# Delta-rule pairs: the sums of squared outputs of two heads as two products with 64 columns of ones, on the two halves of one bank

## The chip, the cores and the metric

The kernel runs on one core of one Trainium2 chip. The metric is the device time of one execution in microseconds (us). PE is TensorE (PEld its weight loads), DVE is VectorE, ACT is ScalarE, POOL is GpSimd, SP is SyncE. Everything is float32 in and out; most weight products are done as three products of rounded high parts and remainders.

## The reference, cut to what matters

The whole program is a transformer block with a state-space mixer, then two blocks with other mixers. The change is in one place of the second part, the gated delta rule (`gdn_mixer`): 8 heads of 128 channels, 512 tokens. After the recurrence each head's output is normalised over its 128 channels, multiplied with a gate, and projected:

```python
def rms_norm_2(x, g):
    xf = x.astype(jnp.float32)
    y = xf * lax.rsqrt(jnp.mean(xf * xf, axis=-1, keepdims=True) + EPS_2)
    return (y * g.astype(jnp.float32)).astype(x.dtype)
...
    o = gated_delta_rule(q, k, v, g, beta).astype(hn.dtype)
    o = rms_norm_2(o, norm_g) * jax.nn.silu(gate)
    return o.reshape(b_, s_, GDN_WIDTH) @ w_out
```

The sum over 128 channels of the squared outputs of a head, its logarithm, and exp(-0.5 log), which is the reciprocal root, are what the change touches.

## The kernel before, in words

Activations stand transposed: 128 channels on the partitions, 512 tokens along the free axis, so one head's output is one 128x512 tile and a sum over channels is a product with a 128x128 matrix of ones, which leaves the sum on all 128 partitions. PSUM `ps` has 8 banks of 128x512 float32. Each engine has its own written instruction list; the engines meet only by semaphores, and each list runs in the order in which it is written.

The delta rule (`pe_mixer2`, `act_mixer2`, `dve_mixer2`, `pool_mixer2`) works on pairs of heads, p = 0 to 3; x = 2p + j is the head. A pair goes through six levels n = 0 to 5 of a triangular inverse, then through four chunks of the recurrence. At each level PE makes the U product (L1514), ACT copies it to `em` (L1732), PE makes the D product (L1549), which has `em` as its weights, and DVE subtracts (L1968) and transposes (L1971). Between these PE does pieces of weight work from a stream (`spare`; L1364 to L1366 for gates, L1375 to L1377 for output parts).

The outputs of pair p end in the banks MOVED = (3, 0). ACT copies each to `v2` (L1778) and squares it into `o_sq[j]` (L1779). The rest belongs to the next pair's levels:

- n = 0: PE multiplies each `o_sq[j]` with 128 columns of ones into bank MOVED[j] (L1520); ACT takes the logarithm back into `o_sq[j]` (L1704, `out_log_sum`), and then casts a weight unit (`act_round`, L413).
- n = 1: PE's transposes of v go into the same banks and wait for the logarithms.
- n = 2: ACT takes the exponential (L1708, `out_rstd`), then scales `kb` (L1719). At n = 3 it copies `em` again.
- n = 3 and 4: DVE uses `o_sq[j]` (L1939, then L1942, `out_gated`).

For the last pair there is no next one, and the same steps stand in a tail: PE L1609, between output products (L1396 to L1398, `pe_out_unit`); ACT a cast L413, L1704, L1708, another cast L413, then `mid2_hi` (L1712); DVE L1939 and L1942 for both heads, then `mid2_lo` (L1947). PE's third output unit of the tail waits for that `mid2_lo`. Whenever ACT has cast a weight unit, POOL computes its remainder (L2639).

`Chain.link(ins)` makes an instruction count on a semaphore of its engine and lets the engine wait for it. The same kernel already has sums with 64 columns of ones for the norms of q and k: `square_sum`, L1446, with ACT's logarithm L1651 and exponentials L1656.

Of the kernel before, what the change touches and what calls it, by code (L numbers as in the profile page):

```python
# [21 lines left out]
ALU, ACT, AX = mybir.AluOpType, mybir.ActivationFunctionType, mybir.AxisListType  # L22

P = 128
# [11 lines left out]
EPS_1, EPS_2 = 1e-5, 1e-6  # L36
# [158 lines left out]
def build(nc, units, x_t, p_t, vectors, constants, rel_table, out_t):  # L195
# [10 lines left out]
    with ExitStack() as ctx:  # L206
# [1197 lines left out]
        def pe_mixer2(pe, w):  # L1404
# [33 lines left out]
            def square_sum(m):  # L1438
# [7 lines left out]
                    last = nc.tensor.matmul(ps[64 * half:64 * half + 64, SUM_BANK[m // 2 % 4], :], ones[:, 0:64], n_sq[:, m % 4 + half, :], start=True, stop=True)  # L1446
                last.then_inc(s_nsum, 2)

            for u in range(N_QKV):
                slot = (n0 + u) % W_SLOTS  # L1450
                pe.wait_ge(s_wlo, n0 + u + 1)
                pe.wait_ge(s_free, b0 + u + 1)
                for k in range(DK):
                    if u == 0:
                        pe.wait_ge(s_xlo, w.tiles - DK + k + 1)
                    hi, lo = w_hi[:, slot, k * P:(k + 1) * P], w_lo[:, slot, k * P:(k + 1) * P]
                    out = ps[:, u % 4, :]
                    nc.tensor.matmul(out, hi, x_hi[:, k, :], start=(k == 0), stop=False)  # L1458
                    nc.tensor.matmul(out, hi, x_lo[:, k, :], start=False, stop=False)  # L1459
                    last = nc.tensor.matmul(out, lo, x_hi[:, k, :], start=False, stop=(k == DK - 1))  # L1460
                last.then_inc(s_used, 1)
                if u == 0:
                    pe_norm_sum(pe, w, 4)
                    pe.wait_ge(s_sum2, 8)
                    nc.tensor.matmul(ps[:, 5, :], ones, sum2[:, :], start=True, stop=True).then_inc(s_msum2, 1)
                    w.norms += 1
                if 5 <= u < 20 and u % 2:
                    if u == 5:
                        pe.wait_ge(s_rstd, w.norms)
                    square_sum(u - 5)  # L1470
                if u == 6:
                    pe.wait_ge(s_ga2, 2)
                    for m in range(NB):
                        last = nc.tensor.transpose(ps[:, 7, m * 64:m * 64 + 40], g_row[:, m * P:(m + 1) * P], ident[0:40, 0:40])
                    last.then_inc(s_gcolp, 1)
                if u == 20:
                    for j in range(2):
                        decay_broadcast(0, j)
                if u == 21:
                    pe.wait_ge(s_nrs, 4)  # L1480
                    nc.tensor.matmul(ps[:, 6, 0:32], ident[:, P - 1:P].to_broadcast([P, P]), cols2[:, :, 0:8], start=True, stop=True).then_inc(s_gtot, 1)
                if u == 22:
                    for j in range(2):
                        beta_broadcast(0, j)
                if u == 23:
                    for j in range(2):
                        products_of_k(0, j)
# [5 lines left out]
            for p in range(4):  # L1493
# [7 lines left out]
                for n in range(6):  # L1501
                    b = 2 << n
                    if n == 5:
                        for j in range(2):
                            pe.wait_ge(s_gd, level(p, 4, j))
                            for c in range(NB):
                                last = nc.tensor.transpose(ps[:, LEVEL[j], c * P:(c + 1) * P], gw["tt"][j][:, c, :], ident)
                            last.then_inc(s_gtp, 1)
                    for j in range(2):
                        pe.wait_ge(s_gao, level(p, n, j))  # L1510
                        pe.wait_ge(s_gtm, level(p, n, j))
                        for c in range(NB):
                            for side in range(2):
                                last = nc.tensor.matmul(level_out(j, 0, b, c, side), gw["ao"][j][:, c, 64 * side:64 * side + 64],  # L1514
                                                        halves(gw["tm"][j][:, c, :], b, 0), start=True, stop=True)
                        last.then_inc(s_gup, 1)
                    if n == 0 and p:
                        for j in range(2):
                            pe.wait_ge(s_osq, 2 * p - 1 + j)
                            nc.tensor.matmul(ps[:, MOVED[j], :], ones, o_sq[j][:, :], start=True, stop=True).then_inc(s_osum, 1)  # L1520
                        spare(stream, "b")
                    for j in range(2):
                        x = 2 * p + j
                        if n == (1 if p else 2):
                            if p:
                                pe.wait_ge(s_oln, x - 1)
                            else:
                                pe.wait_ge(s_free, b0 + 29)
                            for c in range(NB):
                                cols = slice(c * P, (c + 1) * P)  # L1530
                                last = nc.tensor.transpose(ps[:, MOVED[j], cols], v2[:, x, cols], ident)
                            last.then_inc(s_gvt, 1)
                        if n == (2 if p else 3):
                            pe.wait_ge(s_gvb, x + 1)
                            for c in range(NB):
                                cols = slice(c * P, (c + 1) * P)
                                last = nc.tensor.transpose(ps[:, MOVED[j], cols], qk2[:, 8 + x, cols], ident)
                            last.then_inc(s_gkt, 1)
                        if p < 3:
                            if n == 3:  # L1540
                                decay_broadcast(p + 1, j)
                    if n == 1:
                        spare(stream, "U1")
                    for j in range(2):
                        pe.wait_ge(s_gz, level(p, n, j))
                        pe.wait_ge(s_gu, level(p, n, j))
                        for c in range(NB):
                            for side in range(2):
                                last = nc.tensor.matmul(level_out(j, 1, b, c, side), gw["em"][j][:, c, 64 * side:64 * side + 64],  # L1549
                                                        halves(gw["tt"][j][:, c, :], b, 1), start=True, stop=True)  # L1550
                        last.then_inc(s_gdp, 1)
                    spare(stream, f"D{n}")
# [51 lines left out]
            w.square_layer(2)  # L1604
            w.square_layer(2)
            pe_out_unit(pe, n_t, TAIL2[0], (0,), False, mids)
            for j in range(2):
                pe.wait_ge(s_osq, 7 + j)
                nc.tensor.matmul(ps[:, MOVED[j], :], ones, o_sq[j][:, :], start=True, stop=True).then_inc(s_osum, 1)  # L1609
            pe_out_unit(pe, n_t, TAIL2[0], (1, 2, 3), False, mids)  # L1610
            for d in range(2):
                pe.wait_ge(s_fill[d], TASKS_BEFORE[4] // 2)
# [5 lines left out]
        def act_mixer2(act, w, gain):  # L1618
# [80 lines left out]
            def round_at(n):  # L1699
                act_round(act, 0, first + n + AHEAD)  # L1700

            def out_log_sum(p, j):
                act.wait_ge(s_osum, 2 * p + j + 1)
                nc.scalar.activation(o_sq[j][:, :], ps[:, MOVED[j], :], ACT.Ln, bias=EPS_2, scale=1.0 / P).then_inc(s_oln, 1)  # L1704

            def out_rstd(p, j):
                act.wait_ge(s_oln, 2 * p + j + 1)
                nc.scalar.activation(o_sq[j][:, :], o_sq[j][:, :], ACT.Exp, scale=-0.5).then_inc(s_ors, 1)  # L1708

            def out_hi(p, j):  # L1710
                act.wait_ge(s_on, 2 * p + j + 1)
# [11 lines left out]
            for p in range(4):  # L1723
                for n in range(6):
# [7 lines left out]
                        nc.scalar.activation(halves(wide(gw["em"][j]), b, 0), level_out(j, 0, b), ACT.Copy).then_inc(s_gu, 1)  # L1732
                    for j in range(2):
                        x = 2 * p + j
                        if n == 0 and p:
                            out_log_sum(p - 1, j)
                        if n == (1 if p else 2):
                            if x == 0:
                                act.wait_ge(s_convact, 36)
                            act.wait_ge(s_gvt, x + 1)  # L1740
                            for c in range(NB):
                                last = nc.scalar.activation(gw["vb"][j][:, c, :], ps[:, MOVED[j], c * P:(c + 1) * P], ACT.Copy, scale=cols2[:, c, 32 + x:33 + x])
                            last.then_inc(s_gvb, 1)
# [3 lines left out]
                        conv_silu(23)  # L1747
                    if n == 2:
                        if p:
                            for j in range(2):  # L1750
                                out_rstd(p - 1, j)
                            k_scaled(p, 0, "kb", g_exp)
                    if n == 3:
                        if not p:
# [26 lines left out]
            n_t = w.unit  # L1781
            layers = [w.square_layer(2), w.square_layer(2)]
            act_round(act, 0, n_t + AHEAD)
            for j in range(2):
                out_log_sum(3, j)
            for j in range(2):
                out_rstd(3, j)
            act_round(act, 0, n_t + 1 + AHEAD)
            for j in range(2):
                out_hi(3, j)  # L1790
# [1017 lines left out]
```

## Time and profile before

| | |
|---|---|
| time, median of 3 runs | 2560.58 us (2556.51 to 2561.22) |
| the profiled execution's own time | 2560.09 us |
| its span, first to last instruction | 2558.3 us |
| granted TensorE clock, mean | 0.996 |
| PE busy | 2510.6 us, 98% of the span |
| DVE, ACT, POOL busy | 1084.4, 1096.8, 1053.2 us (42%, 43%, 41%) |
| the delta-rule pairs and their tail | about 1225 to 1465 us in the span |

PE is busy nearly always; the other engines are busy less than half the time. Where PE waits, the time is lost; where another engine waits, usually not. A matmul's duration in the rows includes its pipeline, so the distance from start to start is what it costs: weight products of 512 columns follow each other at 0.23 us though each row says 0.39. A float32 product is recorded as two passes, so one instruction with 512 columns gives two rows.

### The profile page before, as it was taken

To read this page: it belongs to the slowest core of one execution; us is meant where nothing else is said; L and a number is where in the kernel's file an instruction comes from. 1 tells how busy PE (TensorE), PEld (TensorE's weight loads), DVE (VectorE), ACT (ScalarE), POOL (GpSimd) and SP (SyncE) were. 2 spreads that over 40 slices of the span, in tenths; PEclk is the share of its full clock that TensorE was granted. 3 is DMA by queue.
4 is the path that set the end of the run, shared out by engine and by line. 5 is a ranking of instruction groups with operands and counts; after the bars stand their busy time and mean duration, and the time that the engine had idled before them with its cause. 6 is when DMAs were issued, how large, how long until landed. Compare 5 with 4: busy or idle time off the path is not lost.

```text
span 2558.3 us, 33981 instructions
## 1 busy us (share of the span) xinstructions
PE 2510.6 (98%) x12682; PEld 2035.4 (80%) x12682; DVE 1084.4 (42%) x1551; ACT 1096.8 (43%) x1619; POOL 1053.2 (41%) x516
## 2 busy tenths in 40 slices
PE   9999999998999999999999999999999999999999
PEld 7888887776888888777778788888877767888887
DVE  4212222978432022498666622022487564211225
ACT  5222232668442222577455632222455684222233
POOL 4444444222444444334444344444444124444444
PEclk9999999999999999999999999999999999999999
DMA  4233332111323333222111133333232113332333
GB/s 159 95 100 98 99 123 91 58 58 50 99 90 99 99 99 99 82 83 84 42 34 35 50 101 96 99 96 101 85 96 83 49 41 108 98 99 91 99 99 115
DMA packets 61726, 222.78 MB, mean 87 GB/s; under 512 B 6704, under 2 KB 6832, under 8 KB 61488
## 3 DMA queue, kind: packets, MB, share of 16 engines
q1 hardware_dynamic: 60928, 218.07, 27.5%
q10 hardware_dynamic: 688, 3.15, 0.4%
q8 instruction: 80, 1.31, 0.2%
q14 instruction: 30, 0.25, 0.0%
HBM read 219.10 MB, written 2.10 MB: 86 GB/s over the span
## 4 chain that ended last, share of the span: by engine, by line
PE 86%; DVE 8%; ACT 4%; issue 2%; DMA 0%; SPq 0%; DVEq 0%; ACTq 0%
PE ps L368 13%; PE ps L370 13%; PE ps L369 13%; PE ps L393 6%; PE ps L395 6%; PE ps L394 6%; PE ps L659 2%; PE ps L660 2%; PE ps L661 2%; PE ps L1458 1%; PE ps L1459 1%; PE ps L1460 1%; PE ps L1514 1%; PE ps L2217 1%; PE ps L875 1%
## 5 line engine op out<-in xcount | busy, mean ns | idle before, releaser
L2639 POOL TENSOR_TENSOR w_lo<-raw,w_hi 128x1024 fp32r<-128x1024 f32 x405 | 990.6, 2448 | 1387.0 <-ACT w_hi L413 1386.8
L413 ACT ACTIVATE w_hi<-raw 128x1024 fp32r<-128x1024 f32 x405 | 425.0, 1051 | 456.7 <-PE ps L395 294.0
L368 PE MATMUL ps<-x_hi,w_hi 128*128 128x512 f32 x1536 | 600.8, 391 | 5.5 <-DVE x_lo L446 5.5
L370 PE MATMUL ps<-x_hi,w_lo 128*128 128x512 f32 x1536 | 597.7, 389 | 0.0
L369 PE MATMUL ps<-x_lo,w_hi 128*128 128x512 f32 x1536 | 597.6, 389 | 0.0
L368 PEld LDWEIGHTS ps<-x_hi,w_hi 128*128 128x128 f32 x1536 | 288.3, 188 | 70.1 <-DVE x_lo L446 7.0
L369 PEld LDWEIGHTS ps<-x_lo,w_hi 128*128 128x128 f32 x1536 | 288.3, 188 | 60.6 <-issue 1.4
L370 PEld LDWEIGHTS ps<-x_hi,w_lo 128*128 128x128 f32 x1536 | 288.3, 188 | 60.2
L393 PE MATMUL ps<-mid_hi,w_hi 128*128 128x512 f32 x736 | 286.3, 389 | 0.0
L394 PE MATMUL ps<-mid_lo,w_hi 128*128 128x512 f32 x736 | 286.3, 389 | 0.0
L395 PE MATMUL ps<-mid_hi,w_lo 128*128 128x512 f32 x736 | 286.3, 389 | 0.0
L540 DVE TENSOR_TENSOR ff_up<-ps,rstd 128x512 f32<-128x512 f32 x88 | 60.8, 691 | 398.5 <-PE ps L370 398.5
L509 ACT ACTIVATE mid_hi<-ff_up 128x512 f32 (+1 forms) x88 | 55.6, 632 | 385.2 <-DVE ff_up L543 385.2
L564 DVE SCALAR_TENSOR_TENSOR h<-ps,h 128x512 f32<-128x512 f32 x64 | 43.7, 689 | 392.3 <-PE ps L395 392.3
L506 ACT ACTIVATE ff_gate<-ff_gate 128x512 f32<-128x512 f32 x88 | 55.6, 632 | 248.1 <-DVE ff_gate L538 248.1
L395 PEld LDWEIGHTS ps<-mid_hi,w_lo 128*128 128x128 f32 x736 | 138.1, 188 | 28.8
L393 PEld LDWEIGHTS ps<-mid_hi,w_hi 128*128 128x128 f32 x736 | 138.1, 188 | 28.6
L394 PEld LDWEIGHTS ps<-mid_lo,w_hi 128*128 128x128 f32 x736 | 138.1, 188 | 28.6
L538 DVE TENSOR_TENSOR ff_gate<-ps,rstd 128x512 f32<-128x512 f32 x88 | 60.8, 691 | 221.9 <-PE ps L370 201.7
L545 DVE TENSOR_TENSOR mid_lo<-ff_up,mid_hi 128x512 f32 x88 | 66.9, 760 | 80.1 <-ACT mid_hi L509 80.1
L659 PE MATMUL ps<-x_hi,w_hi 128*128 128x512 f32 x232 | 92.9, 400 | 0.3 <-DVE x_lo L446 0.3
L661 PE MATMUL ps<-x_hi,w_lo 128*128 128x512 f32 x232 | 90.5, 390 | 0.0
(394 smaller groups left out, 3652.3 us busy)
## 6 DMA issues: line engine op xcount, KB each, us to landing
raw<-in_units_dram SPq DMA_DIRECT2D x406, 512.0 KB, 3.5
h<-in_x_t_dram SPq DMA_DIRECT2D x4, 512.0 KB, 7.1
toep<-in_rel_table_dram ACTq DMA_DIRECT2D x1, 2048.0 KB, 8.9
out_dram<-h SPq DMA_DIRECT2D x4, 512.0 KB, 5.8
p_f<-in_p_t_dram ACTq DMA_DIRECT2D x2, 512.0 KB, 3.6
const<-in_constants_dram SPq DMA_DIRECT2D x1, 832.0 KB, 7.1
vec<-in_vectors_dram SPq DMA_DIRECT2D x1, 137.5 KB, 2.2
```

Of the source, the lines that this page charges most:

```text
L368: nc.tensor.matmul(out, hi, x_hi[:, k, :], start=(k == 0), stop=False)
L369: nc.tensor.matmul(out, hi, x_lo[:, k, :], start=False, stop=False)
L370: last = nc.tensor.matmul(out, lo, x_hi[:, k, :], start=False, stop=(k == DK - 1))
L393: nc.tensor.matmul(out, hi, r_hi, start=(k == 0), stop=False)
L394: nc.tensor.matmul(out, hi, r_lo, start=False, stop=False)
L395: last = nc.tensor.matmul(out, lo, r_hi, start=False, stop=(k == tiles - 1))
L413: nc.scalar.activation(w_hi[:, n % W_SLOTS, :], raw[:, n % RAW_SLOTS, :], ACT.Copy).then_inc(s_whi, 1)
L538: nc.vector.tensor_tensor(ff_gate[:, pair, :], ps[:, 4 * g + j % 4, :], rstd[:, :], ALU.mult).then_inc(s_free, 1)
L545: nc.vector.tensor_tensor(tile_at(mid_lo, done), ff_up[:, pair, :], tile_at(mid_hi, done).bitcast(F32), ALU.subtract).then_inc(s_mlo, 1)
L659: nc.tensor.matmul(out, hi, x_hi[:, k, :], start=(k == 0), stop=False)
L661: last = nc.tensor.matmul(out, lo, x_hi[:, k, :], start=False, stop=(k == DK - 1))
L2639: nc.gpsimd.tensor_tensor(w_lo[:, n % W_SLOTS, :], raw[:, n % RAW_SLOTS, :], w_hi[:, n % W_SLOTS, :].bitcast(F32), ALU.subtract).then_inc( ...
```

## The change

For each pair one semaphore wait on PE asks for both squares; two products with 64 columns of ones put head 0's sum on partitions 0 to 63 and head 1's on partitions 64 to 127 of bank 3. ACT takes one logarithm of the bank. Four exponentials on 64 partitions spread the result: head 1's half to both halves of `o_sq[1]`, head 0's half to both halves of `o_sq[0]`. Two of them are linked, because a later one overwrites what an earlier one reads. Counts on the semaphores are made by two at once. DVE and POOL have the same instructions.

```diff
+            def out_sums(p):
+                pe.wait_ge(s_osq, 2 * p + 2)
+                for j in range(2):
+                    last = nc.tensor.matmul(ps[64 * j:64 * j + 64, MOVED[0], :], ones[:, 0:64], o_sq[j][:, :], start=True, stop=True)
+                last.then_inc(s_osum, 2)
...
                     if n == 0 and p:
-                        for j in range(2):
-                            pe.wait_ge(s_osq, 2 * p - 1 + j)
-                            nc.tensor.matmul(ps[:, MOVED[j], :], ones, o_sq[j][:, :], start=True, stop=True).then_inc(s_osum, 1)
+                        out_sums(p - 1)
                         spare(stream, "b")
...
             pe_out_unit(pe, n_t, TAIL2[0], (0,), False, mids)
-            for j in range(2):
-                pe.wait_ge(s_osq, 7 + j)
-                nc.tensor.matmul(ps[:, MOVED[j], :], ones, o_sq[j][:, :], start=True, stop=True).then_inc(s_osum, 1)
+            out_sums(3)
             pe_out_unit(pe, n_t, TAIL2[0], (1, 2, 3), False, mids)
...
-            def out_log_sum(p, j):
-                act.wait_ge(s_osum, 2 * p + j + 1)
-                nc.scalar.activation(o_sq[j][:, :], ps[:, MOVED[j], :], ACT.Ln, bias=EPS_2, scale=1.0 / P).then_inc(s_oln, 1)
-
-            def out_rstd(p, j):
-                act.wait_ge(s_oln, 2 * p + j + 1)
-                nc.scalar.activation(o_sq[j][:, :], o_sq[j][:, :], ACT.Exp, scale=-0.5).then_inc(s_ors, 1)
+            def out_log_sum(p):
+                act.wait_ge(s_osum, 2 * p + 2)
+                nc.scalar.activation(o_sq[0][:, :], ps[:, MOVED[0], :], ACT.Ln, bias=EPS_2, scale=1.0 / P).then_inc(s_oln, 2)
+
+            def out_rstd(p):
+                act.wait_ge(s_oln, 2 * p + 2)
+                nc.scalar.activation(o_sq[1][0:64, :], o_sq[0][64:128, :], ACT.Exp, scale=-0.5)
+                ch.link(nc.scalar.activation(o_sq[1][64:128, :], o_sq[0][64:128, :], ACT.Exp, scale=-0.5))
+                ch.link(nc.scalar.activation(o_sq[0][64:128, :], o_sq[0][0:64, :], ACT.Exp, scale=-0.5))
+                nc.scalar.activation(o_sq[0][0:64, :], o_sq[0][0:64, :], ACT.Exp, scale=-0.5).then_inc(s_ors, 2)
```

PE's list at level 0 of the second pair, before (`gdn_out_squared` is the semaphore of the squares, s_osq):

```order
L1514 MATMUL ps<-tm1_120,ao1_112 64x64 x7
L1520 MATMUL ps<-o_sq0_133,const_61 128x512 [waits gdn_out_squared]
L1520 MATMUL ps<-o_sq1_134,const_61 128x512 [waits gdn_out_squared]
L1364 MATMUL ps<-x_hi_53,w_hi_50 128x512 [waits spare_bank_free_1,w_lo_ready]
L1365 MATMUL ps<-x_lo_54,w_hi_50 128x512
```

and the same place now:

```order
L1520 MATMUL ps<-tm1_120,ao1_112 64x64 x7
L1452 MATMUL ps<-o_sq0_133,const_61 64x512 [waits gdn_out_squared]
L1452 MATMUL ps<-o_sq1_134,const_61 64x512
L1364 MATMUL ps<-x_hi_53,w_hi_50 128x512 [waits spare_bank_free_1,w_lo_ready]
L1365 MATMUL ps<-x_lo_54,w_hi_50 128x512
```

The second product has no wait of its own any more; the first one waits for both squares.

ACT's list at level 0, before (`gdn_out_squares_summed` is s_osum; L1732 is the copy of `em`, L413 the cast):

```order
L1732 ACTIVATE em0_113<-ps 128x128x2 [waits gdn_u_in_psum]
L1732 ACTIVATE em1_114<-ps 128x128x2 [waits gdn_u_in_psum]
L1704 ACT_TABLE_LOAD
L1704 ACTIVATE o_sq0_133<-ps 128x512 [waits gdn_out_squares_summed]
L1704 ACTIVATE o_sq1_134<-ps 128x512 [waits gdn_out_squares_summed]
L413 ACTIVATE w_hi_50<-raw_49 128x1024 [waits units_used,unit_loaded_0]
```

and now:

```order
L1737 ACTIVATE em0_113<-ps 128x128x2 [waits gdn_u_in_psum]
L1737 ACTIVATE em1_114<-ps 128x128x2 [waits gdn_u_in_psum]
L1706 ACT_TABLE_LOAD [waits gdn_out_squares_summed]
L1706 ACTIVATE o_sq0_133<-ps 128x512
L413 ACTIVATE w_hi_50<-raw_49 128x1024 [waits units_used,unit_loaded_0]
```

One logarithm is gone, and the wait for the sums now stands at the table load of the logarithm, which before had no wait in front of it. In the tail the rows are the same, with a cast L413 in place of the copies of `em`.

ACT's list at level 2, before (`gdn_out_log_sums` is s_oln, L1719 the scaling of `kb`):

```order
L1732 ACTIVATE em0_113<-ps 128x32x8 [waits gdn_u_in_psum]
L1732 ACTIVATE em1_114<-ps 128x32x8 [waits gdn_u_in_psum]
L1708 ACT_TABLE_LOAD
L1708 ACTIVATE o_sq0_133<-o_sq0_133 128x512 [waits gdn_out_log_sums]
L1708 ACTIVATE o_sq1_134<-o_sq1_134 128x512 [waits gdn_out_log_sums]
L1719 ACTIVATE kb0_121<-ps,g_exp_103 128x128 [waits gdn_k_by_token_in_psum,gdn_all_columns]
```

and now:

```order
L1737 ACTIVATE em0_113<-ps 128x32x8 [waits gdn_u_in_psum]
L1737 ACTIVATE em1_114<-ps 128x32x8 [waits gdn_u_in_psum]
L1710 ACT_TABLE_LOAD
L1710 ACTIVATE o_sq1_134<-o_sq0_133 64x512 [waits gdn_out_log_sums]
L1711 ACTIVATE o_sq1_134<-o_sq0_133 64x512
L1712 ACTIVATE o_sq0_133<-o_sq0_133 64x512 [waits scalar_steps]
L1713 ACTIVATE o_sq0_133<-o_sq0_133 64x512 [waits scalar_steps]
L1724 ACTIVATE kb0_121<-ps,g_exp_103 128x128 [waits gdn_k_by_token_in_psum,gdn_all_columns]
```

Two exponentials became four, and the last two each wait for the one before (`scalar_steps`). The scaling of `kb`, and behind it the copies of `em` of level 3, stand behind all four.

## Rows read from the trace of the kernel before

**Rows 1.** The page: busy time by engine; costliest groups (busy, mean ns | idle).

```profile
PE 2510.6 (98%) x12682; PEld 2035.4 (80%) x12682; DVE 1084.4 (42%) x1551; ACT 1096.8 (43%) x1619; POOL 1053.2 (41%) x516
...
L2639 POOL TENSOR_TENSOR w_lo<-raw,w_hi 128x1024 fp32r<-128x1024 f32 x405 | 990.6, 2448 | 1387.0 <-ACT w_hi L413 1386.8
```

**Rows 2.** PE timeline: start us, us, engine line; level 0 of pair 1, tail.

```profile
1286.53 2.04 PE L1520 MATMUL ps<-o_sq,const 128*128 128x512 f32 x4
...
1288.64 0.39 PE L1365 MATMUL ps<-x_lo,w_hi 128*128 128x512 f32 x1
...
1444.39 0.40 PE L1397 MATMUL ps<-mid_lo,w_hi 128*128 128x512 f32 x1
```

**Rows 3.** PEld timeline: weight loads of head 1's sum, pair 1 and tail.

```profile
1287.45 0.30 PEld L1520 LDWEIGHTS ps<-o_sq,const 128*128 128x128 f32 x2 [0.62 <-ACT o_sq L1779]
...
1443.16 0.33 PEld L1609 LDWEIGHTS ps<-o_sq,const 128*128 128x128 f32 x2 [0.53 <-ACT o_sq L1779]
```

**Rows 4.** PE timeline: a pair of sums with 64 columns of ones.

```profile
1102.30 1.08 PE L1446 MATMUL ps<-n_sq,const 128*64 128x512 f32 x4
...
1103.64 0.39 PE L1459 MATMUL ps<-x_lo,w_hi 128*128 128x512 f32 x1
```

**Rows 5.** ACT timeline: levels 0 to 3 of pair 1.

```profile
1287.25 0.71 ACT L1732 ACTIVATE em<-ps 128x256 f32<-128x256 f32 x2
...
1287.99 1.28 ACT L1704 ACT_TABLE_LOAD   x1
...
1289.28 1.09 ACT L1704 ACTIVATE o_sq<-ps 128x512 f32<-128x512 f32 x2
...
1290.25 1.06 ACT L413 ACTIVATE w_hi<-raw 128x1024 fp32r<-128x1024 f32 x1
...
1300.94 1.15 ACT L1708 ACTIVATE o_sq<-o_sq 128x512 f32<-128x512 f32 x2
...
1302.00 1.12 ACT L1719 ACTIVATE kb<-ps,g_exp 128x128 f32<-128x128 f32 x4
...
1303.06 0.38 ACT L1732 ACTIVATE em<-ps 128x256 f32<-128x256 f32 x1
```

**Rows 6.** ACT timeline: whole and half tiles; two copies that wait.

```profile
1121.20 1.01 ACT L1651 ACTIVATE ps<-ps 128x1024 f32<-128x1024 f32 x1
...
1123.52 4.12 ACT L1656 ACTIVATE n_rs<-ps 64x1024 f32<-64x1024 f32 x4
...
1128.96 0.63 ACT L1662 ACTIVATE qk<-cv 128x512 f32<-128x512 f32 x1
...
1129.62 0.64 ACT L1696 ACTIVATE n_sq<-qk 128x512 f32<-128x512 f32 x1
```

**Rows 7.** ACT timeline: `em` at level 3 of pair 3.

```profile
1410.85 0.39 ACT L1732 ACTIVATE em<-ps 128x256 f32<-128x256 f32 x1
```

**Rows 8.** PE timeline: the D products of level 3, pairs 1 and 3.

```profile
1304.52 1.15 PE L1549 MATMUL ps<-tt,em 128*64 128x64 f32 x32
...
1411.59 1.45 PE L1549 MATMUL ps<-tt,em 128*64 128x64 f32 x32
```

**Rows 9.** The chain that ended last, in the tail: start us, us, what.

```profile
1444.07 1.28 ACT L1704
...
1446.46 1.28 ACT L1708
...
1448.42 0.76 DVE v L1939
...
1450.60 2.77 DVE v L1942
```

**Rows 10.** ACT timeline: the tail's exponentials and cast.

```profile
1448.82 1.04 ACT L413 ACTIVATE w_hi<-raw 128x1024 fp32r<-128x1024 f32 x1
```

**Rows 11.** POOL timeline: the remainder behind that cast.

```profile
1449.94 2.89 POOL L2639 TENSOR_TENSOR w_lo<-raw,w_hi 128x1024 fp32r<-128x1024 f32 x1 [3.41 <-ACT w_hi L413]
```

**Rows 12.** PE timeline: first product of the tail's third unit.

```profile
1454.12 0.47 PE L1396 MATMUL ps<-mid_hi,w_hi 128*128 128x512 f32 x1 [0.23 <-DVE mid_lo L1947]
```

More of the change, by code:

```diff
@@ L1734, in act_mixer2 @@
                         x = 2 * p + j
-                        if n == 0 and p:
-                            out_log_sum(p - 1, j)
+                        if n == 0 and p and j == 0:
+                            out_log_sum(p - 1)
                         if n == (1 if p else 2):
@@ L1749, in act_mixer2 @@
                         if p:
-                            for j in range(2):
-                                out_rstd(p - 1, j)
+                            out_rstd(p - 1)
                             k_scaled(p, 0, "kb", g_exp)
@@ L1783, in act_mixer2 @@
             act_round(act, 0, n_t + AHEAD)
[L1784 to L1787, printed above, removed]
+            out_log_sum(3)
+            out_rstd(3)
             act_round(act, 0, n_t + 1 + AHEAD)
```

## The prediction, word for word

> **What bounds the kernel now.** I read the page first, then the timelines of each engine at the four places where the sums stand, then the chain of waits in the tail. The page has PE busy for 98% of the span and ACT for 43% [rows 1]. So a microsecond less on PE counts, a microsecond more on ACT counts only where PE then waits. The timelines answer two questions: how long PE spends on the sums, and how much slack there is behind ACT's part.
>
> The four places are level 0 of pairs 1, 2 and 3, and the tail. At each the sums are four passes (two products, two passes each). In pair 1 they start at 1286.53 us, and head 1's weights are loaded at 1287.45, the moment its square is there: the row names ACT as what ended the idle time [rows 2, 3]. So before, PE used that wait for head 0's passes. That is the key to the change: the new order gives up this cover.
>
> **PE's part.** The kernel already holds the new form: `square_sum` makes two sums with 64 columns of ones on the two halves of a bank. Its four passes take 1.08 us in all, from 1102.30, and the second weight product behind them starts 1.34 us after their start [rows 4]. Four passes one after the other with 128 columns have a row of 2.04 us [rows 2], so the halves do overlap. But now the first product waits for both squares (PE's order: the one wait stands at the first product). The start is therefore head 1's moment, 1287.45, not 1286.53. From there:
> - before: 1287.45 to the second weight product behind the sums, L1365 at 1288.64, is 1.19 us [rows 2, 3]; in the tail 1443.16 to 1444.39 is 1.23 us;
> - after: 1.34 us from the same moment [rows 4].
> That is +0.15 us in each pair and +0.11 us in the tail. The saved passes are spent waiting. Bounds: if the products overlapped better than in rows 4 I can gain at most some 0.3 us a place; if they did not overlap at all each place costs some 0.9 us more. I take the rows, since form, length and operands are the same.
>
> **ACT's logarithm.** Before, the table load ran at 1287.99 straight behind the copies of `em` and the logarithms followed at 1289.28 [rows 5]. Now the load stands behind the wait. The sums are done at 1287.45 + 1.08 = 1288.53; load 1.28, then one logarithm of some 0.6 (two overlapped take 1.09): done at 1290.45. Two logarithms ended at 1290.37. The exposed load and the missing logarithm cancel to 0.1 us, and behind them is only the cast L413, 1.06 us long [rows 5], which nobody at this level waits for; the next level's copies and PE's transposes come behind two more products of a level. I cost this at nothing in the three pairs; the price would show if the sums came some 2 us later.
>
> **ACT's exponentials.** Two whole tiles took from 1300.94 to 1302.00, where `kb` starts: 0.53 us each [rows 5]. Half the partitions are not half the time: 64x1024 takes 4.12 / 4 = 1.03 us, 128x1024 1.01 us [rows 6]. So four exponentials are four of the old size. Two follow without a wait (0.53 each), two wait for the one before; for that I take the step of a copy that waits for its forerunner, 1128.96 to 1129.62 = 0.66 us [rows 6]. Start of the first to start of `kb`: 0.53 + 0.66 + 0.66 + 0.53 = 2.38 us instead of 1.06, so +1.32 us. Bounds: 0 if half tiles were half price, some +1.9 if every one had to drain and signal dearly. `kb` and the first `em` of level 3 are queued behind, and PE's D product of level 3 waits for `em`:
> - pair 1: `em` starts at 1303.06 + 1.32 = 1304.38, takes 0.38, ends 1304.76. PE comes at 1304.52 + 0.15 = 1304.67 [rows 5, 8]. Late by 0.1 us. Pair 2 has the same spacing; I take 0.05.
> - pair 3: there is no next pair, so PE has less work in between and comes sooner. `em` starts at 1410.85 + 1.32, ends 1412.56; the D products start then instead of at 1411.59. Their row was 1.45 us, with a gap before head 1's half; in pair 1 without gap 1.15 [rows 7, 8]. End: about 1412.6 + 1.15 = 1413.75 instead of 1413.04, so +0.7 us, of which 0.15 is counted above: +0.55.
> DVE needs the exponentials only behind its subtractions and transposes of level 3, so behind the D product of 1304.52 [rows 8], over 1 us after they are done (about 1303.4 now): nothing.
>
> **The tail.** Here nothing covers ACT: the chain of waits runs through table load, logarithm, table load, exponentials, DVE's two steps [rows 9]. New times: sums done 1443.16 + 1.08 = 1444.24; load to 1445.55 (before it began at 1444.07 without waiting); logarithm to 1446.15; load to 1447.45; exponentials start there and end at 1447.45 + 0.53 + 0.66 + 0.66 + 0.62 = 1449.92. DVE's L1939 begins at 1449.95 instead of 1448.42: +1.5 us. What comes then is set by POOL. The cast behind the exponentials started at 1448.82 [rows 10], POOL's remainder at 1449.94 for 2.89 us, to 1452.83 [rows 11]; DVE's second L1942, begun 1450.60, lasted 2.77 us to 1453.37, that is until 0.54 us after POOL was done, where the L1939 of the same size took 0.76 [rows 9]. So DVE is held while POOL runs. Now the cast starts at 1447.45 + 2.38 = 1449.83, POOL asks at 1450.95, in the middle of DVE's first L1942, and gets its 2.45 us [rows 1] from about 1451.4 to 1453.85. DVE's second L1939 is held to 1454.4, its L1942 ends at 1455.1. Before, from 1453.37 to PE's product at 1454.12 were 0.75 us, and PE had already been idle for 0.23 [rows 12]. Now PE goes on at 1455.85: +1.7 us, with the 0.11 in it. Bounds: if POOL and DVE miss each other, DVE ends at some 1452.9 and PE waits for nothing, which gives back the idle 0.23: -0.1 us; a hold more would be +2.5. I take +1.7.
>
> The Trainium skill ("ScalarE: Activation LUTs", section "What ACT_TABLE_LOAD costs") has a rule against this change: a switch of table costs about 2.66 us, load and drain. This trace differs: the load of 1287.99, 1.28 us long, ends at 1289.27 and the logarithm starts at 1289.28 [rows 5], with no further gap. By the page the exposed load of the tail would cost 1.38 us more, and the time would be 2564.3.
>
> **Sum.** 3 x 0.15 + 0.1 + 0.05 + 0.55 + 1.7 = +2.85 us. Against the profiled execution's own 2560.09 (span 2558.3 and 1.8 around it) that is 2562.9; against the median of 2560.58 it is 2563.4. I say 2563.1. A measurement of this kernel can tell about 0.2%, 5.1 us, from no change, so this is no change that can be told.
>
> **Rivals.**
> - The saving stands: squares come early enough and PE gains the overlap of all four places, 0.85 us each (two of four passes of 0.43), and the tail is hidden: -3.4 us, 2556.7. Against it: PE's idle row that ends with ACT's square [rows 3]. Also the case in which ACT's half tiles are cheap. Chance 0.09.
> - The tail misses POOL: 3 x 0.15 + 0.7 - 0.1 = +1.05 us, 2561.1. For it: the meeting depends on half a microsecond. Against it: both DVE and POOL are released by the same run of ACT, so their distance is set, and POOL's request falls inside DVE's four steps. Chance 0.20.
> - Slower: ACT's block of exponentials becomes the bound. It stands ahead of the `em` of level 3 in three pairs and of DVE's steps in the tail, so every 0.1 us that it takes beyond 2.38 costs nearly 0.1 at four places. From 0.55 us more (a wait for the forerunner that costs some 0.4 instead of 0.13) the sum passes +5.1 us. With 0.85 us more it is 2.85 + 3.4 = +6.3 us, 2566.4. For it: in pair 3 there is no slack at all [rows 7, 8]. Against it: the step of 0.66 in rows 6. Chance 0.13.
> - The halves do not overlap: 4 x 0.9 = +3.6 on top, 2566.7. Against it: rows 4. Chance 0.03.
> - The page's table rule: 2564.3. The trace speaks against it; chance 0.02.
>
> **How the numbers follow.** The forecast has 0.53; its own range is 2560.5 to 2565.5, from the sizes of the waits and the spread of the runs. The median of three runs has itself an error of about 2 us (2556.51 to 2561.22 before). The range of 8 in 10 takes in the missed meeting with POOL and part of both ends: 2557.5 to 2567.0. Faster by over 0.2% needs a gain of 5.1 us, more than the first rival gives: 0.05. Slower by over 0.2%: most of the slower rivals and an edge of the forecast, 0.17. Within 0.2%: 0.78.
>
> **What would show it.** On PE, idle time before the first sum that ends with ACT's square, about 0.8 us in the pairs, then four passes in 1.1 us. On ACT, a table load that starts only after the sums, and a block of exponentials of 2.4 us; in the tail DVE's first L1939 1.5 us later against the squares, and one DVE step of over 2 us behind POOL. In pair 3 PE's level-3 D product after `em`, some 0.7 us late. Wrong would be: exponentials of 64 partitions at 0.3 us, a product that starts before both squares, a step between linked exponentials of over 0.9 us, or a total beyond 5 us either way.

## The result and the profile after

The changed kernel takes 2561.8 us (median of 12 runs, 2559.02 to 2564.98), the kernel before 2556.58 us (median of 12, 2554.19 to 2561.22). The ratio of the times is 1.0019, with a 95% interval of 1.001 to 1.0027: 2.6 to 6.9 us slower. That lies in the range forecast, has the sign of the forecast, and is larger than the +2.85 us of its sum. The kernel before stood at 2560.58 us when the forecast was made, the median of three runs; its median of 12 is 4.0 us lower.

The two profiled executions say the opposite at first sight: spans of 2557.2 us after and 2558.3 us before. The reason lies outside the change. PE's granted clock falls to its lower level (1.2 instead of 2.4 GHz) for short stretches, and which of them appear differs from one trace to the next. The view by stretches (busy time of PE, PEld, DVE, ACT, POOL, then PEclk, DMA share, GB/s) of the kernel before:

```profile
630.00:660.00 30.00, 26.90 (x143) 20.39 (x143) 16.80 (x19) 19.53 (x37) 10.34 (x5) 0.94 0.23 71
1215.00:1280.00 65.00, 58.30 (x618) 49.61 (x616) 40.47 (x64) 29.16 (x68) 30.91 (x36) 0.92 0.13 41
1280.00:1470.00 190.00, 184.23 (x1931) 150.67 (x1931) 125.09 (x208) 106.80 (x229) 75.45 (x86) 1.00 0.13 40
```

and the same stretches after:

```profile
630.00:660.00 30.00, 27.96 (x154) 22.07 (x151) 19.24 (x21) 18.70 (x31) 12.07 (x5) 1.00 0.28 80
1215.00:1280.00 65.00, 58.35 (x648) 49.76 (x647) 40.09 (x63) 25.20 (x62) 28.55 (x33) 0.95 0.11 34
1280.00:1470.00 190.00, 176.85 (x1885) 143.66 (x1881) 122.16 (x203) 110.66 (x234) 72.87 (x85) 1.00 0.12 37
```

Around 630 to 660 us, where nothing was changed, the clock is 0.94 in one and 1.00 in the other. The last stretch, with all four changed places, has 1.00 in both, so there the two traces can be laid side by side. I took the start of the same PE instruction in both and subtracted. Just before the first sums (L1364, 1280.96 before) the trace after is 6.03 us early; that is the zero. Most of it, 5.5 us, comes about between 621 and 645 us, far ahead of the change, where the clock is low twice in the kernel before (at 621 and 642 us) and not at all in the one after. From there the lag grows as follows, and the same is done for every experiment below; in none of their traces does the clock fall between there and the end of the tail.

| lag of PE in us, at | after |
|---|---|
| pair 1: sums; level 3 | 0.16; 0.65 |
| pair 2: sums; level 3 | 0.80; 1.29 |
| pair 3: sums; level 3 | 1.48; 2.45 |
| tail: sums; third unit | 2.59; 4.34 |

So each place with sums adds 0.14 to 0.19 us, level 3 adds 0.49, 0.49 and 0.97 us, the tail 1.75 us. In all 4.34 us, inside the interval of the timed runs. Who PE waited for in the delta rule and its tail (1281 to 1466 us) after: us in total, times, longest:

```profile
PE ps L1452 <- ACT o_sq L1783: 3.0, 4, 0.8
PE ps L1396 <- DVE mid_lo L1949: 2.0, 1, 2.0
PE ps L1553 <- ACT em L1737: 1.9, 3, 1.1
```

In the kernel before, PE's matmuls have neither the first nor the third of these waits (only the weight load of head 1's sum waited, under head 0's passes [rows 3]), and the second was 0.2 us [rows 12]. Line numbers are moved by the change: L1452 is the new sum, L1553 the D product, L1737 the copy of `em`, L1941 and L1944 DVE's steps of before at L1939 and L1942.

PE at the sums and at level 3 of pair 1, and at level 3 of pair 3, after:

```profile
1281.42 1.08 PE L1452 MATMUL ps<-o_sq,const 128*64 128x512 f32 x4 [0.84 <-ACT o_sq L1783]
1282.43 0.50 PE L1364 MATMUL ps<-x_hi,w_hi 128*128 128x512 f32 x1
1282.76 0.39 PE L1365 MATMUL ps<-x_lo,w_hi 128*128 128x512 f32 x1
...
1299.14 1.15 PE L1553 MATMUL ps<-tt,em 128*64 128x64 f32 x32 [0.42 <-ACT em L1737]
...
1408.31 1.15 PE L1553 MATMUL ps<-tt,em 128*64 128x64 f32 x32 [1.08 <-ACT em L1737]
```

The four passes take 1.08 us and the second weight product comes 1.34 us after their start, exactly as in [rows 4]. Each pass is 0.59 to 0.64 us long; the first passes of the two products start at 1281.42 us, under 0.01 us apart, the second ones at 1281.90: the two halves run at the same time. The 0.84 us of waiting ahead of them eats what they save against [rows 2]. The D products, which waited for nothing before [rows 8], now wait for `em`.

ACT in pair 1, after:

```profile
1281.22 0.71 ACT L1737 ACTIVATE em<-ps 128x256 f32<-128x256 f32 x2
1282.59 1.28 ACT L1706 ACT_TABLE_LOAD   x1 [0.65 <-PE ps L1452]
1283.88 0.60 ACT L1706 ACTIVATE o_sq<-ps 128x512 f32<-128x512 f32 x1
...
1295.06 0.63 ACT L1710 ACTIVATE o_sq<-o_sq 64x512 f32<-64x512 f32 x1
1295.70 0.63 ACT L1711 ACTIVATE o_sq<-o_sq 64x512 f32<-64x512 f32 x1
1296.37 0.63 ACT L1712 ACTIVATE o_sq<-o_sq 64x512 f32<-64x512 f32 x1
1297.09 0.63 ACT L1713 ACTIVATE o_sq<-o_sq 64x512 f32<-64x512 f32 x1
1297.62 1.10 ACT L1724 ACTIVATE kb<-ps,g_exp 128x128 f32<-128x128 f32 x4
1298.62 0.64 ACT L1737 ACTIVATE em<-ps 128x256 f32<-128x256 f32 x2
```

The table load stands behind a wait of 0.65 us and follows the sums. The steps of the exponentials are 0.64, 0.67, 0.72 and 0.53 us, 2.56 us to `kb`, where [rows 5] had 1.06. The first `em` is done at about 1299.0 and PE starts at 1299.14.

The chain of waits in the tail, after:

```profile
1440.78 1.28 ACT L1706
...
1442.07 0.60 ACT o_sq L1706
...
1442.68 1.28 ACT L1710
...
1446.67 0.76 DVE v L1941
...
1448.07 2.90 DVE v L1941
...
1450.99 0.69 DVE v L1944
...
1452.43 0.47 PE ps L1396
```

Against [rows 9] it is DVE's second L1941 that is held, no longer its second L1944. POOL's remainder at that time:

```profile
1447.66 2.74 POOL L2641 TENSOR_TENSOR w_lo<-raw,w_hi 128x1024 fp32r<-128x1024 f32 x1 [4.70 <-ACT w_hi L413]
```

It ends at 1450.40, and DVE's step at 1450.97, as with [rows 11].

### The profile page after: what moved, and what is told of

It is laid out like the page before. It is cut to its first block, busy times and chain, and to the rows that moved or that the text cites. A ratio compares the mean times of both kernels' runs of the same rounds, so it can differ in the third digit from the quotient of the medians.

```text
span 2557.2 us, 33993 instructions
## 1 busy us (share of the span) xinstructions
PE 2505.1 (98%) x12682; PEld 2032.7 (79%) x12682; DVE 1083.7 (42%) x1551; ACT 1099.7 (43%) x1623; POOL 1052.3 (41%) x516
## 4 chain that ended last, share of the span: by engine, by line
PE 87%; DVE 7%; ACT 4%; issue 2%; DMA 0%; SPq 0%; DVEq 0%; ACTq 0%
PE ps L368 13%; PE ps L369 13%; PE ps L370 13%; PE ps L393 6%; PE ps L395 6%; PE ps L394 6%; PE ps L659 2%; PE ps L660 2%; PE ps L661 2%; PE ps L1464 2%; PE ps L1466 2%; PE ps L1465 2%; PE ps L2219 1%; PE ps L2221 1%; PE ps L2220 1%
## 5 line engine op out<-in xcount | busy, mean ns | idle before, releaser
L413 ACT ACTIVATE w_hi<-raw 128x1024 fp32r<-128x1024 f32 x405 | 425.1, 1051 | 454.4 <-PE ps L395 289.2
```

The costliest lines, as they stand in the source:

```text
L413: nc.scalar.activation(w_hi[:, n % W_SLOTS, :], raw[:, n % RAW_SLOTS, :], ACT.Copy).then_inc(s_whi, 1)
```

## The experiments

Lags are PE's, in us against the kernel before, taken as above from L1364 ahead of pair 1's sums on (two columns for a pair: behind the sums, behind level 3).

Each kernel has one trace. A ratio, where one is given, is to runs of the kernel before that were timed beside it, with its 95% interval.

| kernel | pair 1 | pair 2 | pair 3 | tail: sums; third unit |
|---|---|---|---|---|
| after | 0.16; 0.65 | 0.80; 1.29 | 1.48; 2.45 | 2.59; 4.34 |
| two whole exponentials | 0.17; 0.17 | 0.35; 0.34 | 0.52; 0.51 | 0.65; 1.12 |
| half exponentials alone | -0.01; 0.49 | 0.61; 1.12 | 1.10; 2.11 | 2.13; 4.21 |
| one wait alone | 0.86; 0.87 | 1.72; 1.72 | 2.58; 2.57 | 3.39; 3.00 |
| early load | 0.17; 0.66 | 0.78; 1.28 | 1.46; 2.43 | 2.56; 4.04 |
| old tail | 0.14; 0.63 | 0.78; 1.27 | 1.37; 2.35 | 2.33; 2.33 |
| later sums | -0.93; -0.43 | -1.38; -0.88 | -1.73; -0.75 | -0.77; -0.76 |
| split exponentials | -0.92; -0.92 | -1.83; -1.83 | -2.69; -2.69 | -2.72; -2.72 |
| half tiles by rows | 0.00; 0.31 | 0.33; 0.64 | 0.65; 1.45 | 1.45; 3.19 |

**Two whole exponentials.**

```diff
-                nc.scalar.activation(o_sq[1][0:64, :], o_sq[0][64:128, :], ACT.Exp, scale=-0.5)
-                ch.link(nc.scalar.activation(o_sq[1][64:128, :], o_sq[0][64:128, :], ACT.Exp, scale=-0.5))
-                ch.link(nc.scalar.activation(o_sq[0][64:128, :], o_sq[0][0:64, :], ACT.Exp, scale=-0.5))
-                nc.scalar.activation(o_sq[0][0:64, :], o_sq[0][0:64, :], ACT.Exp, scale=-0.5).then_inc(s_ors, 2)
+                ch.link(nc.scalar.activation(o_sq[1][:, :], o_sq[0][:, :], ACT.Exp, scale=-0.5))
+                nc.scalar.activation(o_sq[0][:, :], o_sq[0][:, :], ACT.Exp, scale=-0.5).then_inc(s_ors, 2)
```

> The changed kernel with two exponentials of whole tiles in place of the four of half tiles, in the pairs and in the tail. It leaves out the sorting of the two heads' sums: each head is normalised with a mixture of both. PE's products are the changed kernel's. Theory A (the block of exponentials ahead of the level-3 copies of em is what costs PE most): the level-3 losses (0.50, 0.50 and 0.97 us in the profile after) go to 0, the losses at the sums stay at 0.14 to 0.19 us each, and the tail falls from 1.75 to about 0.4 us, since the exponentials end 1.3 us sooner and DVE meets POOL in the same way; in all PE is some 1.0 us later than before instead of 4.3. Rival B (the new products and PE's wait cost it): PE stays over 3 us later.

Measured: +1.12 us on PE, of which level 3 has none and the tail behind its sums 0.47. Ratio 1.0005 (0.9995 to 1.0015). Theory A holds, rival B falls: the new products, wait and all, cost 0.65 us at four places. The tail of this run:

```profile
1444.71 0.63 ACT L1710 ACTIVATE o_sq<-o_sq 128x512 f32<-128x512 f32 x1
1445.43 0.63 ACT L1711 ACTIVATE o_sq<-o_sq 128x512 f32<-128x512 f32 x1
```

```profile
1447.50 2.89 DVE L1939 SCALAR_TENSOR_TENSOR v<-v,vec,o_sq 128x512 f32<-128x512 f32 x1
```

The second exponential starts 0.72 us after the first, whose end it waits for. A step of DVE is held here too, as in the kernel before and in the changed one.

**Half exponentials alone.** In the kernel before:

```diff
             def out_rstd(p, j):
-                act.wait_ge(s_oln, 2 * p + j + 1)
-                nc.scalar.activation(o_sq[j][:, :], o_sq[j][:, :], ACT.Exp, scale=-0.5).then_inc(s_ors, 1)
+                if j:
+                    return
+                act.wait_ge(s_oln, 2 * p + 2)
+                nc.scalar.activation(o_sq[1][0:64, :], o_sq[1][0:64, :], ACT.Exp, scale=-0.5)
+                ch.link(nc.scalar.activation(o_sq[1][64:128, :], o_sq[1][64:128, :], ACT.Exp, scale=-0.5))
+                ch.link(nc.scalar.activation(o_sq[0][64:128, :], o_sq[0][64:128, :], ACT.Exp, scale=-0.5))
+                nc.scalar.activation(o_sq[0][0:64, :], o_sq[0][0:64, :], ACT.Exp, scale=-0.5).then_inc(s_ors, 2)
```

> The kernel before with its old products and two logarithms, but with four exponentials of half tiles, linked as in the change, each in place. The values are the same as before. Theory A: nothing is lost at the sums, 0.5, 0.5 and 1.0 us at level 3 of the three pairs, and in the tail DVE starts 2.0 us later (two logarithms, block of 2.56 us), PE about 2 us later: +4.0 us in all, as much as the whole change. Rival B: under 1 us in all. On the step between the first two, which have no wait between them: 0.53 us as for whole tiles if half tiles overlap like whole ones, 0.64 us as in the profile after if half tiles on different partitions, or instructions without a count, do not overlap.

Measured: +4.21 us, as much as the whole change, with PE's products untouched. Ratio 1.0017 (1.0007 to 1.0027). The steps were 0.65, 0.66, 0.72 and 0.54 us. Together with the run before it this settles the main question: most of the time goes to ACT's exponentials, through `em` at level 3 and through the tail. That both totals are so close is chance in part: 2.02 us are lost at level 3, as in the change (1.95), nothing at the sums, and 2.08 in the tail instead of 1.75, because this kernel keeps its second logarithm; 0.1 more comes behind level 3 of pair 1.

**One wait alone.** In the kernel before, both `pe.wait_ge(s_osq, ...)` ahead of the sums ask for both squares:

```diff
-                            pe.wait_ge(s_osq, 2 * p - 1 + j)
+                            pe.wait_ge(s_osq, 2 * p)
...
-                pe.wait_ge(s_osq, 7 + j)
+                pe.wait_ge(s_osq, 8)
```

> The kernel before with one edit: both products with 128 columns wait for both squares. Theory A (before, head 0's passes covered the wait for head 1's square): idle time of 0.8 us on PE ahead of the sums and then four passes of 0.43 us one after the other, so 0.9 us are lost in each pair and some 0.6 in the tail, +3.3 us in all. If the wait is hidden otherwise: 0. The difference to the 0.15 us of the change is what the overlapping halves give, 0.75 us a place.

PE in pair 1 of this run:

```profile
1284.55 1.99 PE L1520 MATMUL ps<-o_sq,const 128*128 128x512 f32 x4 [0.84 <-ACT o_sq L1779]
1285.97 0.79 PE L1364 MATMUL ps<-x_hi,w_hi 128*128 128x512 f32 x1
1286.61 0.39 PE L1365 MATMUL ps<-x_lo,w_hi 128*128 128x512 f32 x1
```

Measured: 0.86 us in each pair, 0.82 at the tail's sums, +3.00 us in all (one profile); 0.39 us of the lag is gone again at the third unit, where PE was waiting before too. L1365 comes 2.06 us after the sums' start; with the halves in the change it is 1.34 us. So the overlap is worth 0.72 us a place, and the lost cover costs 0.86.

**Early load.** The changed kernel, with `s_oln` counted by one (the three waits for it, not shown, are changed to match):

```diff
-                nc.scalar.activation(o_sq[0][:, :], ps[:, MOVED[0], :], ACT.Ln, bias=EPS_2, scale=1.0 / P).then_inc(s_oln, 2)
+                nc.scalar.activation(o_sq[0][:, :], ps[:, MOVED[0], :], ACT.Ln, bias=EPS_2, scale=1.0 / P).then_inc(s_oln, 1)
```

> The changed kernel with counts made by one on the semaphore of the logarithms (and the waits for them changed to match), so that the wait stays with the logarithm and the table load stands ahead of it without a wait, as before. Theory A: no gain in the pairs, since nobody waits for the logarithm there; in the tail the load starts 0.3 us sooner, at the end of the cast, and all behind it follows, so PE is 0.3 us less late: +4.0 instead of +4.3 us. Rival C (the exposed load is what the tail lost): 1.3 us less late.

Measured: +4.04 us, 0.30 less than after, all of it in the tail (one profile). ACT in the tail of this run:

```profile
1441.33 1.08 ACT L413 ACTIVATE w_hi<-raw 128x1024 fp32r<-128x1024 f32 x1
1442.42 1.28 ACT L1706 ACT_TABLE_LOAD   x1
1443.71 0.60 ACT L1706 ACTIVATE o_sq<-ps 128x512 f32<-128x512 f32 x1
```

The load follows the cast without a wait. Rival C falls: in the change the wait held the load up by 0.29 us only. In the kernel before the load did not start until the cast was done either, at 1444.07 [rows 9].

**Old tail.** The changed kernel, with the tail's sums, logarithms and exponentials of the kernel before:

```diff
-            out_sums(3)
+            for j in range(2):
+                pe.wait_ge(s_osq, 7 + j)
+                nc.tensor.matmul(ps[:, MOVED[j], :], ones, o_sq[j][:, :], start=True, stop=True).then_inc(s_osum, 1)
...
-            out_log_sum(3)
-            out_rstd(3)
+            for j in range(2):
+                act.wait_ge(s_osum, 7 + j)
+                nc.scalar.activation(o_sq[j][:, :], ps[:, MOVED[j], :], ACT.Ln, bias=EPS_2, scale=1.0 / P).then_inc(s_oln, 1)
+            for j in range(2):
+                act.wait_ge(s_oln, 7 + j)
+                nc.scalar.activation(o_sq[j][:, :], o_sq[j][:, :], ACT.Exp, scale=-0.5).then_inc(s_ors, 1)
```

> The changed kernel with the tail of the kernel before (two products with 128 columns, two logarithms, two exponentials), the pairs as changed. Theory A: the pairs lose what they lost, +2.45 us up to the tail, and the tail loses nothing: DVE's first L1939 again 5.3 us after the last square and PE idle 0.2 us ahead of the third unit, +2.45 us in all. If the tail's loss came from the pairs' delay, it stays at 4.3 us.

Measured: +2.33 us, none of it in the tail. Ratio 1.0013 (1.0002 to 1.0023). The tail's loss is its own.

**Later sums.** The old tail, and in the pairs:

```diff
-                        out_sums(p - 1)
                         spare(stream, "b")
+                        out_sums(p - 1)
...
                         if n == 0 and p and j == 0:
+                            round_at(3 * p)
                             out_log_sum(p - 1)
...
-                    if n == 0:
+                    if n == 0 and not p:
                         round_at(3 * p)
```

> As the run with the old tail, and in the pairs PE does its two pieces of weight work (1.4 us) ahead of the sums instead of behind them, ACT its cast ahead of the logarithm. Theory A: both squares are there when PE comes, so no idle time and the overlapping halves pay: some 1.1 us for the sums instead of 1.8, -0.65 us in each pair against the kernel before; level 3 still loses 0.5, 0.5 and 1.0 us; in all 0.0 +- 0.3 us. Rival: the later logarithm holds up the copies of em of level 1 or the transposes of v, and the sums gain nothing: +2 us.

Measured: -0.93, -0.95 and -0.85 us at the sums, +0.50, +0.50 and +0.98 at level 3, -0.76 us in all. Ratio 0.9993 (0.9982 to 1.0004). The sums gain more than I had worked out. The 1.1 us was the length of their row, and what counts is the distance to the next product: 0.91 us to the D product behind them (rows below), 1.01 to the weight product in the change. That this distance is shorter because the D product has 64 columns as the sums have is likely, but not shown. Level 3 is as it was in the change.

**Split exponentials.** As the run with the later sums, and one of the four at level 1:

```diff
             def out_rstd(p):
                 act.wait_ge(s_oln, 2 * p + 2)
-                nc.scalar.activation(o_sq[1][0:64, :], o_sq[0][64:128, :], ACT.Exp, scale=-0.5)
...
+            def out_rstd_first(p):
+                act.wait_ge(s_oln, 2 * p + 2)
+                nc.scalar.activation(o_sq[1][0:64, :], o_sq[0][64:128, :], ACT.Exp, scale=-0.5)
...
+                    if n == 1 and p:
+                        out_rstd_first(p - 1)
```

> As the run with the later sums, and the table load and the first exponential stand at level 1 behind the scaling of v, where ACT is idle for 2.3 us; three exponentials stay at level 2. Theory A: kb and em of level 3 then come 0.5 us sooner than before the change, level 3 loses nothing, and only the gain at the sums is left: -2.0 to -2.3 us against the kernel before, PE ahead of the old times from the first sums on; the ratio of times 0.999. Rival: ACT's level 1 is not idle enough and level 2 loses what level 3 gains: 0.

PE and, below, ACT of this run in pair 1:

```profile
1288.00 1.08 PE L1452 MATMUL ps<-o_sq,const 128*64 128x512 f32 x4
1288.91 1.11 PE L1553 MATMUL ps<-tt,em 128*64 128x64 f32 x32
...
1303.49 1.15 PE L1553 MATMUL ps<-tt,em 128*64 128x64 f32 x32
```

```profile
1295.51 1.28 ACT L1718 ACT_TABLE_LOAD   x1
1296.80 0.63 ACT L1718 ACTIVATE o_sq<-o_sq 64x512 f32<-64x512 f32 x1
1297.74 0.85 ACT L1742 ACTIVATE em<-ps 128x256 f32<-128x256 f32 x2 [0.31 <-PE ps L1520]
1298.62 0.63 ACT L1712 ACTIVATE o_sq<-o_sq 64x512 f32<-64x512 f32 x1
```

Measured: level 3 loses nothing, -2.72 us in all, more than the 2.0 to 2.3 worked out, as the sums gain 0.92, 0.91 and 0.86 us; ratio 0.9986 (0.9978 to 0.9995), median 2555.64 us (12 runs) beside 2558.06 us of the kernel before (29 runs). ACT waits 0.31 us even at level 2, so the load and one exponential fit into its idle time. This version is faster than the kernel before by 0.05 to 0.22%; it was not timed beside the changed one, whose own ratio is 1.0019. It has the old tail: what later sums would do there was not tried.

**Half tiles by rows.** In the kernel before:

```diff
             def out_rstd(p, j):
-                act.wait_ge(s_oln, 2 * p + j + 1)
-                nc.scalar.activation(o_sq[j][:, :], o_sq[j][:, :], ACT.Exp, scale=-0.5).then_inc(s_ors, 1)
+                if j:
+                    return
+                act.wait_ge(s_oln, 2 * p + 2)
+                nc.scalar.activation(o_sq[1][0:64, :], o_sq[1][0:64, :], ACT.Exp, scale=-0.5)
+                nc.scalar.activation(o_sq[0][0:64, :], o_sq[0][0:64, :], ACT.Exp, scale=-0.5)
+                nc.scalar.activation(o_sq[0][64:128, :], o_sq[0][64:128, :], ACT.Exp, scale=-0.5)
+                nc.scalar.activation(o_sq[1][64:128, :], o_sq[1][64:128, :], ACT.Exp, scale=-0.5).then_inc(s_ors, 2)
```

> The kernel before with four exponentials of half tiles in place and no waits between them: first rows 0 to 63 of both tiles, then rows 64 to 127 of both. It measures the step. If a half tile never overlaps with the next instruction, all three steps are 0.64 us; if only a change of rows between two instructions costs the overlap, the first and third step are 0.53 and the second 0.64 us. PE at level 3: late by some 0.3 us in pairs 1 and 2 and by 0.8 in pair 3.

ACT in pair 1 of this run:

```profile
1304.39 0.63 ACT L1710 ACTIVATE o_sq<-o_sq 64x512 f32<-64x512 f32 x1
1304.92 0.62 ACT L1711 ACTIVATE o_sq<-o_sq 64x512 f32<-64x512 f32 x1
1305.55 0.63 ACT L1712 ACTIVATE o_sq<-o_sq 64x512 f32<-64x512 f32 x1
1306.09 0.61 ACT L1713 ACTIVATE o_sq<-o_sq 64x512 f32<-64x512 f32 x1
1306.72 1.14 ACT L1724 ACTIVATE kb<-ps,g_exp 128x128 f32<-128x128 f32 x4
```

Steps of 0.53, 0.63, 0.54 and 0.63 us: it is the change of rows that costs 0.1 us, not the half tile. What counts is the row at which the output begins. The last step goes from rows 64 to 127 to all rows of `kb` and takes 0.63 us; in the change the last exponential is on rows 0 to 63, and the same step takes 0.53; there, too, the first two exponentials read the same rows, write different ones, and are 0.64 us apart. PE lost 0.31, 0.31 and 0.80 us at level 3 (one profile), 0.2 us less at each than with the links of the run with half exponentials, where the block is 2.56 us long instead of 2.33.

## Why the prediction was right, and where it was too small

- **What bounds.** Right: PE's waits set the result, and the three waits that appeared are those named.
- **The sums.** Right to 0.05 us: 0.16, 0.15, 0.19 and 0.14 us measured for 0.15, 0.15, 0.15 and 0.11. The reason was shown from both sides: the lost cover costs 0.86 us (one wait alone), the overlap gives back 0.72.
- **The logarithm.** Right: the load moved behind the wait, and in the pairs nobody waited. The run with the early load shows the price of the wait ahead of the load: 0.30 us, in the tail.
- **The exponentials at level 3.** The mechanism was right, the size was not. This is the term that was mis-sized: 0.1 + 0.05 + 0.55 = 0.70 us forecast, 0.49 + 0.49 + 0.97 = 1.95 us measured. Three things were missing in each pair, about 0.4 us together. First, I let PE come 0.15 us later for the sums but left ACT's times at their old place; ACT's level 2 follows PE, so it was late by the same 0.15 us and that was no slack. Second, I let PE start when `em` ended, where the rows show some 0.14 us from ACT's end to PE's start. Third, the block to `em` came out 0.12 us longer than forecast (2.56 us of exponentials for 2.38, `kb` a little shorter). With these, pair 1 comes to 0.1 + 0.41 = 0.51 us, pair 3 to 0.55 + 0.41 = 0.96 us.
- **The tail.** Right to 0.16 us: 1.75 us behind the sums, for 1.7 with the sums in it, that is 1.59 without. DVE's first step came 1.81 us later against the last square (7.12 us behind its end, 5.31 before), not 1.5; less of that reached PE, since DVE's second step ends with POOL either way. The meeting with POOL came as described, with DVE's second L1939 (now L1941) held to 0.57 us after POOL's end. What is too small is again the block of exponentials. DVE was held in the kernel before, in the changed one and in the run with two whole exponentials, where PE was only 0.47 us late; at what distance the two would miss each other is not shown.
- **The sum.** 2.85 us forecast, 4.34 us on PE in one trace, 5 us (2.6 to 6.9) timed. The excess in the trace is 1.25 us from level 3 and 0.2 from the rest. That the absolute time came out so near, 2561.8 us for 2563.1, is luck in part: the base was 3.7 us too high and the difference 2.4 us too small. From the median of 12 runs the same sum gives 2559.4. The rivals' times start from 2560.1 or, with the sum in them, from 2562.9 in one place and 2563.1 in another, which is 0.2 us of difference.
- **The rivals.** The slower one, ACT's block as the bound, was the direction in which the forecast erred, though not by its threshold of 0.55 us: the block was 0.18 us longer, and the rest was slack that did not exist. That the halves do not overlap fell (1.08 us for four passes). That the tail misses POOL fell as well (DVE's step of 2.90 us). That the saving stands fell for this order; with the sums behind the weight work 0.9 us a place is saved in the pairs. The rule of the Trainium skill ("ScalarE: Activation LUTs", section "What ACT_TABLE_LOAD costs"), 2.66 us for a switch, is not borne out: the load at 1282.59 is 1.28 us long and the logarithm starts at 1283.88, 1.29 us after it. Nor would 1.38 us have been the right charge: the tail has the same two loads before and after, both in the chain of waits, so that a fixed price for each would be in both times.

## What to carry to other kernels

A cheaper product on the busy engine gains nothing if it waits longer for its operand than it saves: look at what the old one did while it waited, and put independent work there first (here that turned +0.15 us a place into -0.93). Count what a merge adds on the engine behind it, in instructions and not in bytes, and follow that engine's queue to the next thing that the busy engine needs. When one engine's times are shifted in a forecast, shift those of the engines that follow it too, and only then read the slack.

## What the runs showed that I had not expected

- An activation of 512 columns whose output begins at another row than that of the one before does not overlap with it: 0.63 us from start to start instead of 0.53, with no wait between them (half tiles by rows). With a link to the one before the step is 0.66 us where the wait sits on the instruction and 0.72 where it stands by itself, also with whole tiles on the same rows (two whole exponentials). It stood by itself wherever the waiting instruction counts by two.
- The same holds for the table load: with a count of two on the logarithm the wait is written ahead of the load, with a count of one behind it (early load).
- The stretches of lower granted clock come near a few places (about 622, 642, 1215, 1240, 1260 and 2105 us, and in three of the ten traces at 10 us), but not at all of them in every trace, and shift the whole program by more than this change does (5.5 us by 645 us, 4.34 for the change). The runs of the changed kernel, too, have mean granted clocks from 0.996 to 0.999. Timed runs could tell the sign of the larger differences; the lags of single places came only from a stretch at full clock on both sides.
